# Attention scores of three heads as three rounded passes, in a two-layer streaming encoder

## The reference

```python
mk, mv = jnp.split(mem @ xa_w_kv, 2, axis=-1)
xa = memory_attention(heads(a_q, XA_HEADS), heads(mk, XA_HEADS), heads(mv, XA_HEADS))

def memory_attention(q, mk, mv):
    s = jnp.einsum('blhd,bmhd->bhlm', q, mk).astype(jnp.float32) * XA_DH ** -0.5
    p = jax.nn.softmax(s, -1)
    return jnp.einsum('bhlm,bmhd->blhd', p, mv.astype(jnp.float32))
```

## Time and profile before

| | us |
|---|---|
| median of 3 runs | 1762.28 |
| lowest, highest | 1760.89, 1763.03 |
| the profiled execution | 1758.43 |
| its span, first to last instruction | 1756.4 |

### The profile page before, as it was taken

The page is one execution under the profiler, slowest core; times in us unless marked ns, Lnnn a source line. Parts: engine busy times, 40 slices in busy tenths (PEclk is TensorE's granted clock), DMA queues, the critical chain, the costliest instruction groups (busy, mean ns, idle before and its releaser), DMA issues.

```text
span 1756.4 us, 22844 instructions
## 1 busy us (share of the span) xinstructions
PE 1727.4 (98%) x8848; PEld 1437.9 (82%) x8848; DVE 1040.9 (59%) x2022; ACT 595.2 (34%) x829; POOL 542.0 (31%) x342
## 2 busy tenths in 40 slices
PE   7999999999999999999999999999999999999998
PEld 6888888887787888888898888788878878888886
DVE  8898736572392587249747887353624825862625
ACT  5333244541125114332243332544311341143320
POOL 2544412022113213345456342211212141324451
PEclk9999999999999999999999999999999999999999
DMA  7344355051032206764343443541411232258441
GB/s 295 136 129 127 110 205 179 37 156 49 25 108 108 96 29 242 257 240 170 120 153 118 120 122 105 207 176 54 128 35 49 97 114 78 82 218 302 153 172 56
DMA packets 98707, 235.23 MB, mean 134 GB/s; under 512 B 10912, under 2 KB 41968, under 8 KB 97064
## 3 DMA queue, kind: packets, MB, share of 16 engines
q1 hardware_dynamic: 71688, 182.15, 30.8%
q10 hardware_dynamic: 26832, 51.39, 8.1%
q0 software_dynamic: 80, 0.23, 0.0%
HBM read 170.55 MB, written 58.98 MB: 131 GB/s over the span
## 4 chain that ended last, share of the span: by engine, by line
PE 93%; DVE 3%; ACT 2%; issue 1%; DMA 0%; ACTq 0%; SPq 0%; DVEq 0%
PE gp L629 22%; PE gp L631 22%; PE gp L630 22%; PE mm L630 3%; PE mm L631 3%; PE mm L629 3%; PE mm L861 2%; PE mm L839 2%; PE mm L784 1%; PE mm L885 1%; PE mm L786 1%; PE mm L785 1%; PE mm L1012 1%; PE mm L932 1%; PE mm L849 1%
## 5 line engine op out<-in xcount | busy, mean ns | idle before, releaser
L1152 POOL TENSOR_TENSOR wlo<-wraw,whi 128x256 fp32r<-128x256 f32 (+1 forms) x270 | 448.3, 1686 | 993.0 <-ACT whi L1230 993.0
L629 PE MATMUL gp<-xh,whi 128*128 128x512 f32 x768 | 318.2, 414 | 1.4 <-ACT xh L1300 1.4
L631 PE MATMUL gp<-xh,wlo 128*128 128x512 f32 x768 | 300.8, 392 | 0.0
L630 PE MATMUL gp<-xl,whi 128*128 128x512 f32 x768 | 299.6, 390 | 0.0
L629 PE MATMUL gp<-whi,xh 128*128 128x512 f32 x640 | 269.6, 421 | 0.0
L1230 ACT ACTIVATE whi<-wraw 128x1024 fp32r<-128x1024 f32 x164 | 168.2, 1054 | 267.4 <-DMA wraw<-in_w 113.0
L631 PE MATMUL gp<-whi,xl 128*128 128x512 f32 x640 | 250.6, 392 | 0.0
L630 PE MATMUL gp<-wlo,xh 128*128 128x512 f32 x640 | 250.0, 391 | 0.0
L631 PEld LDWEIGHTS gp<-xh,wlo 128*128 128x128 f32 x768 | 144.1, 188 | 31.9
L629 PEld LDWEIGHTS gp<-xh,whi 128*128 128x128 f32 x768 | 144.5, 188 | 30.2 <-issue 3.1
L630 PEld LDWEIGHTS gp<-xl,whi 128*128 128x128 f32 x768 | 144.8, 189 | 25.9
(11 more groups left out here) (335 smaller groups left out, 2936.0 us busy)
## 6 DMA issues: line engine op xcount, KB each, us to landing
wraw<-in_w SPq DMA_DIRECT2D x164, 512.0 KB, 4.1
spill<-gate ACTq DMA_DIRECT2D x32, 512.0 KB, 3.1
yraw<-yt SPq DMA_DIRECT2D x32, 512.0 KB, 5.3
xs<-xr SPq DMA_DIRECT2D x16, 512.0 KB, 5.4
xraw<-in_xT SPq DMA_DIRECT2D x4, 1024.0 KB, 17.2
ud<-gate ACTq DMA_DIRECT2D x8, 512.0 KB, 2.6
uu<-ud SPq DMA_DIRECT2D x64, 64.0 KB, 2.6
p_tab<-kd SPq DMA_DIRECT2D x64, 64.0 KB
```

The costliest lines, as they stand in the source:

```text
L629: nc.tensor.matmul(out, ah, bh, start=start, stop=False)
L630: nc.tensor.matmul(out, ah, bl, start=False, stop=False)
L631: return nc.tensor.matmul(out, al, bh, start=False, stop=stop)
L1152: last = nc.gpsimd.tensor_tensor(wlo[slot(u)][:, w0 + c:w0 + c + n], raw_view(l, u, i)[:, c:c + n], whi[slot(u)][:, w0 + c:w0 + c + n].bit ...
```

## The change

For heads 1 to 3 the scores are made with `mm3` from split queries and keys, six rounded matmuls a step instead of two plain ones; head 0 stays as it was. The splitting is new work: ScalarE makes the rounded keys of three heads (`mkh`) and the rounded queries (`aqh`) in `x_high`, GpSimd the rests (`mkl`, `aql`) in `query_lo`, in pieces of 256 columns. `x_high(1)` stands ahead of hook 0, `x_high(2)` behind hook 9, `x_high(3)` behind hook 16. On GpSimd the rests of the keys and of head 1 stand between the two halves of the rests of unit `U_QK + 1`, those of heads 2 and 3 behind them. TensorE waits at each head's first scores for `xq_lo`. Two semaphores are merged with others (`mk_in` into `aq_in0`, `wif_lo` into `x_norm`). The loads stay where they were.

```diff
@@ scores, TensorE
-                    if j % 8 == 0:
-                        pe.wait_ge(aq_in[j // 8], 32 * l + 32)
+                        pe.wait_ge(aq_in[0], 48 * l + 48)
+                    elif t == 0:
+                        pe.wait_ge(S["xq_lo"], 4 * l + h + 1)
...
-                        last = nc.tensor.matmul(bank[j % 2][:, 256 * c:256 * c + 256], aq[h][:, a0:a0 + 128], mkT[:, NMEM * h:NMEM * h + NMEM],
-                                                start=True, stop=True)
+                        o, m0 = bank[j % 2][:, 256 * c:256 * c + 256], NMEM * h
+                        if h:
+                            last = mm3(o, aqh[h - 1][:, a0:a0 + 128], aql[h - 1][:, a0:a0 + 128], mkh[:, m0:m0 + NMEM], mkl[:, m0:m0 + NMEM],
+                                       True, True)
+                        else:
+                            last = nc.tensor.matmul(o, aq[h][:, a0:a0 + 128], mkT[:, m0:m0 + NMEM], start=True, stop=True)
@@ rests, GpSimd
+            def query_lo(l, n):
+
+                pool.wait_ge(S["xq_hi"], 4 * l + n + 1)
+                c0 = 0 if n else NMEM
+                raw_, hi, low = (aq[n], aqh[n - 1], aql[n - 1]) if n else (mkT, mkh, mkl)
+                for c in range(c0, T, 256):
+                    last = nc.gpsimd.tensor_tensor(low[:, c:c + 256], raw_[:, c:c + 256], hi[:, c:c + 256].bitcast(F32), ALU.subtract)
+                last.then_inc(S["xq_lo"], 1)
...
-                for u in range(U_RZ + 1, U_LO):
+                for u in range(U_RZ + 1, U_QK + 1):
+                    lo(l, u)
+                lo(l, U_QK + 1, (0,))
+                for n in range(4):
+                    query_lo(l, n)
+                    if n == 1:
+                        lo(l, U_QK + 1, (1,))
+                for u in range(U_RV, U_LO):
                     lo(l, u)
@@ rounded halves, ScalarE
+                def x_high(h):
+                    if h == 1:
+                        act.wait_ge(aq_in[0], 48 * l + 48)
+                        F(mkh[:, NMEM:], mkT[:, NMEM:], ACT.Copy).then_inc(S["xq_hi"], 1)
+                    elif h == 2:
+                        act.wait_ge(aq_in[1], 32 * l + 32)
+                    F(aqh[h - 1], aq[h], ACT.Copy).then_inc(S["xq_hi"], 1)
...
+                x_high(1)
                 for w, u in enumerate((U_QK, U_QK + 1)):
                     for i in range(16):
                         attend(16 * w + i)
+                        if 16 * w + i in (9, 16):
+                            x_high(2 + w)
```

More of the change, by code:

```diff
@@ L242, in build @@
         aq = [at(f"aq{h}", T, (R[0] + 2048, R[0] + 3072, o_v, o_v + 1024)[h]) for h in range(HEADS)]
+        aqh = [at(f"aqh{h}", T, R[2] + T * h, F32R) for h in range(1, HEADS)]
+        aql = [at(f"aql{h}", T, (R[0] + 3072, o_v, o_v + 1024)[h - 1], F32R) for h in range(1, HEADS)]
         mkT, mvT = at("mkT", 1024, o_ys), at("mvT", 1024, R[3])
+        mkh, mkl = at("mkh", 1024, R[2], F32R), at("mkl", 1024, o_ys, F32R)
         pm = [at(f"pm{i}", 512, R[3] + 1024 + 512 * i) for i in range(2)]
@@ L267, in build @@
             sp_out0 sp_out1 gate_in0 gate_in1 gate_used0 gate_used1 rt_done rt_free yt_out0 yt_out1 yt_out2 yt_out3
-            mt_done mt_free mk_in mv_in aq_in0 aq_in1 xo_out xo_in ring_in ring_used
+            mt_done mt_free mv_in xq_hi xq_lo aq_in0 aq_in1 xo_out xo_in ring_in ring_used
             x_s x_max x_e x_norm x_t x_pt x_pv x_pvev xa_out wif_in
-            wif_hi wif_lo if_done if_act if_sum rows_done rf_out ab_in wa_ev res_in colt_done cols_done wqk_in conv_done xc_ready
+            wif_hi if_done if_act if_sum rows_done rf_out ab_in wa_ev res_in colt_done cols_done wqk_in conv_done xc_ready
             ones_done w_arg w_exp w_mask qk_mm qk_ev s_mm s_w k_tr k_w m_num m_read m_c m_st m_h gn_in uu_in0 uu_in1 yc_in0 yc_in1 yc_in2 yc_in3
@@ L491, in _ @@
                     sp.dma_start(aq[h], dram["spill"][D_AQ + h]).then_inc(aq_in[0], 16)
-                sp.dma_start(mkT, dram["kvs"][:, 0:1024]).then_inc(S["mk_in"], 16)
+                sp.dma_start(mkT, dram["kvs"][:, 0:1024]).then_inc(aq_in[0], 16)
                 raw(l, U_GL + 2)
@@ L828, in x_scores @@
                     if j == 0:
-                        pe.wait_ge(S["mk_in"], 16 * l + 16)
                         pe.wait_ge(S["p_ev"], NPB * l + NPB)
@@ L838, in x_scores @@
                         a0 = 256 * t + 128 * c
-                        last = nc.tensor.matmul(bank[j % 2][:, 256 * c:256 * c + 256], aq[h][:, a0:a0 + 128], mkT[:, NMEM * h:NMEM * h + NMEM],
-                                                start=True, stop=True)
+                        o, m0 = bank[j % 2][:, 256 * c:256 * c + 256], NMEM * h
[4 more added lines that the diff above has]
+                            last = nc.tensor.matmul(o, aq[h][:, a0:a0 + 128], mkT[:, m0:m0 + NMEM], start=True, stop=True)
                     last.then_inc(S["x_s"], 1)
                 def x_turn(j):
-                    pe.wait_ge(S["x_norm"], XSTEPS * l + j + 1)
+                    pe.wait_ge(S["x_norm"], (XSTEPS + 1) * l + j + 1)
                     if j:
@@ L878, in _ @@
                 pe.wait_ge(S["wif_hi"], l + 1)
-                pe.wait_ge(S["wif_lo"], l + 1)
+                pe.wait_ge(S["x_norm"], (XSTEPS + 1) * (l + 1))
                 pe.wait_ge(S["x_pt"], XSTEPS * l + XSTEPS)
@@ L2057, in _ @@
                 TT(wv[:, :, 64:128], wifr.rearrange("p (k c) -> p k c", k=KT)[:, :, 0:64], wv[:, :, 0:64].bitcast(F32),
-                   ALU.subtract).then_inc(S["wif_lo"], 1)
+                   ALU.subtract).then_inc(S["x_norm"], 1)
                 dve.wait_ge(g_free[0], units_to(l, U_QK + 1))
```

## The result

The changed kernel takes 1771.6 us (median of 5 runs, 1769.25 to 1774.01), the kernel before 1762.28 (5 runs, 1760.89 to 1765.83): a ratio of 1.0054 [1.0042, 1.0066], 9.3 us slower. The forecast was slower by 4.4 us, 1766.7. The sign was right; the size is more than double, and the time lies 0.6 us above the range.

The account below looks back on a forecast made before the run. TensorE, busy 98% of 1756.4 us, was taken to bound the kernel. Two waits, +6.9 us, less 2.5 us from 18 steps of faster passes, gave +4.4 us on 1762.28: 1766.7 us, range 1763 to 1771.

Parts of the forecast that it names:

- Passes: Scores of heads 1 to 3 on TensorE: six rounded passes of 0.12 us, 0.72 a step, gaining 0.14 us a step.
- rival 2: Rounded passes on TensorE run at the plain rate, 0.1075 us, a step gains 0.215: +3.0 us, 1765.3; chance 0.08.
- The wait and its chain: ScalarE's copy behind hook 9 waits for query loads, delaying exponential, `xo` and TensorE's values of step 3: 6.9 us together.
- Rival 1: The wait at the copy behind hook 9 does not reach TensorE: 3.4 us faster, 1758.9; chance 0.07.
- Nothing in the change moves these loads: SyncE's loads of the queries of heads 2 and 3 keep their issue times, 296.7 and 297.2, landing at 303.3.
- done by 286: GpSimd's seven new early pieces of 0.7 us end by 286, well before the unit's rests at 293.4.
- rival 3: The wait lowers TensorE's clock: 2.0 us after each of both waits, +8.4 us, 1770.7; chance 0.13.
- Everything else on ScalarE, GpSimd and the later heads: ScalarE's other copies, GpSimd's 15 pieces a layer and the scores of heads 2 and 3 cost nothing.
- second wait: Sign against the forecast: another wait of TensorE in hooks 13 to 22; none was expected there.
- The sum: Whole kernel: +6.9 us for two waits, less 2.5 for 18 steps behind them, +4.4 us, median 1766.7.

Follow-up runs that it names:

- few rests: Changed kernel without GpSimd's first seven pieces in their early place (five not made, two moved behind the unit's rests; head 1 uses rounded halves): 1767.09 us.
- copy alone: Kernel before plus only ScalarE's copy of head 2's queries behind hook 9, with its wait for their loads; nobody reads the copy: ratio 1.0054.
- Splitting alone: Changed kernel with query loads of heads 2 and 3 early and plain matmuls for heads 1 to 3: 0.9 us faster than the kernel before.
- three mended kernels: Changed kernel with query loads ahead of the weight load, with head 2's copy behind hook 11, or with both: 6.5 to 6.9 us below the kernel before.
- Passes alone: Kernel before with heads 1 to 3 scored in six rounded passes a step over tiles already there, nothing split: ratio 0.9975.

## Why the prediction was right or wrong

- **Passes: right.** 0.12 us each, 0.72 a step; behind the wait part C and the step in B give back 1.24 + 0.15 = 1.4 us a layer, where 9 x 0.14 = 1.26 were forecast. The bound of 0.1075 (rival 2) falls.
- **The wait and its chain: right.** Place, releaser and the order of what is queued behind the copy are as forecast. Rival 1 falls. With the loads where they were, its price is right too: values of step 3 3.3 us late in "few rests" and "copy alone", 3.4 forecast.
- **"Nothing in the change moves these loads": this step failed.** They were issued 1.5 us later, since GpSimd's seven pieces, costed at nothing and "done by 286", lay until 288.4 beside VectorE's softmax of steps 0 and 1, slowed it, and were slowed by it. The prediction asked only whether GpSimd would be done in time, not whom it slows. Counted in A, 4.82 us late instead of 3.4; worth 3.0 us in two layers, and 5.3 with the clock (81.66 - 79.03 and 81.54 - 78.86). Row and rule agree here: the Trainium skill (SBUF — State Buffer, section Who interferes with whom) says that VectorE shares a pair of ports with GpSimd: an operation on two SBUF inputs contends there with GpSimd's reads, a `TENSOR_SCALAR` can, and a reduction does not. In the trace the products and the scaling are longer, and the maximum is not. The prediction should have weighed this rule, and the row of 0.51 us at 294.34.
- **The clock: rival 3 came in, under the forecast's own wait.** "Few rests" has a wait of 3.57 us, nearly the 3.7 that rival 3 spoke of, and the clock falls, for 1.6 us a layer against 2.0 priced. So the clock was not a case beside the forecast but its consequence, and a chance of 0.13 was far too low. In the changed kernel it cost 2.75 and 2.5. The Trainium skill (TensorE: Matmul & The Clock Gate, section HAM oscillation — how this bites in real kernels) says that a TensorE that waits between bursts starts the next one throttled; the trace agrees in both layers, with a clock of 0.51 behind the wait.
- **Everything else on ScalarE, GpSimd and the later heads: right.** "Splitting alone" bounds it at 0.13 us a layer. No second wait appeared in hooks 13 to 22.
- **The sum.** Forecast per layer: +3.4 wait, -1.26 passes. Found in the first layer: +4.82 in A, +2.75 clock, -1.4 passes, so +6.17; in the second +6.05; together 12.2 us in the traces. Of these, 6.9 are there without GpSimd's early pieces ("few rests": the forecast's wait and passes, and the clock), and 5.3 come with them. The medians differ by 9.3. That this lies so near rival 3's +8.4 is in part luck: its sum has nothing of the later loads, and the medians show 3 us less than the stage.

**What stays open.** The medians of the three mended kernels lie 6.5 to 6.9 us below the kernel before, where their traces of the stage show 3.2 to 3.5; that of the changed kernel 9.3 above, where they show 12.2. Outside the stage the traces differ by up to 5.7 us (the span less both stages: 1604.4 to 1610.1), and no one line accounts for it, so some 3 us in favour of the kernels that have both passes and splitting are not explained. "Passes alone" (4.8 us faster by the medians) and "splitting alone" (0.9) hint that they are not the work of one part. No run here settles it; the changed kernel's loss lies in the stage.

## What to carry to other kernels

Ahead of any instruction that is put on an in-order engine, ask when its inputs land; if that is a load issued late, put the load earlier or the instruction behind whatever the bottleneck needs next (each alone turned +9 us into a gain here). Price a new wait of TensorE with the clock behind it, not by its length alone. And work that "fits into idle time" of GpSimd is not free while VectorE works on SBUF beside it: look at whose chain those instructions are.

## What was not expected of the hardware

In "copy alone" the clock fell a third time, behind a wait of only 1.92 us in another place. It fell at 1134.3, when TensorE had been at work again for 1.3 us, and until 1137.7 a matmul of 512 columns cost 0.43 us instead of 0.23, some 1.7 us in all by estimate (half of the 3.4):

```profile
1132.99 0.47 PE L630 MATMUL gp<-yh,whi 128*128 128x512 f32 x1 [1.92 <-DVE yl L1999]
...
1136.03 0.63 PE L632 MATMUL gp<-yh,wlo 128*128 128x512 f32 x1
1136.45 0.63 PE L630 MATMUL gp<-yh,whi 128*128 128x512 f32 x1
```

The wait of 1.7 us in the kernel before, at the same place, left it at 1.00; what decides between the two is not shown. And the low stretch was not of one length: 3.4 us with the waits of 3.2 and 3.6 us, 6.8 with those of 5.0, of which the first 1.1 (first layer) lay still in the wait: the 0.90 of its row above.
